# A two-block transformer on one core: GpSimd makes the gate's remainders between the strip transfers

## The reference, cut to what matters

```python
    u = u_tab[e]
    a = jax.nn.gelu(jnp.einsum('pd,phkd->phk', xb, u).astype(jnp.float32), approximate=False)
    return jnp.einsum('phk,phkd->pd', g * a, v_tab[e].astype(jnp.float32)).astype(xb.dtype)
```

## Time and profile before

| | |
|---|---|
| three runs | 3113.87 us median (3100.89 to 3116.61) |
| the profiled execution | 3107.74 us, of which the span is 3106.1 us |
| granted TensorE clock, mean | 0.951 of full |
| busy in the span | PE 92%, DVE 64%, ACT 34%, POOL 28% |
| stage V of layer 0, 727 to 1203 us | PE busy 456.8 of 476 us, DVE 384.7, POOL 45.6 |

### The profile page before, as it was taken

How to read it: one execution, slowest core, us unless ns; L and a number is a source line. 1 busy time by engine, 2 the same in 40 slices (tenths; PEclk the granted TensorE clock), 3 DMA queues, 4 the chain that set the end, 5 groups by cost and what they waited for, 6 DMA issues and landing times.

```text
span 3106.1 us, 54274 instructions
## 1 busy us (share of the span) xinstructions
PE 2857.3 (92%) x20018; PEld 2589.8 (83%) x20018; DVE 1981.1 (64%) x2912; ACT 1048.4 (34%) x1508; POOL 867.7 (28%) x521
## 2 busy tenths in 40 slices
PE   4989999999999988889999999999898879978798
PEld 4459999999999987669999999999896459855696
DVE  6433986777988766426967768997772349132690
ACT  1214443333333333224443333333342124321443
POOL 2006991000000110037970000001110029900596
PEclk9989999999999989889999999999998989987899
DMA  8524554445666874244554445667882335531454
GB/s 326 184 88 151 180 178 153 140 141 180 203 195 229 286 272 165 68 133 155 180 174 141 139 149 191 200 203 262 281 279 100 102 109 176 190 114 36 134 181 145
DMA packets 147037, 536.77 MB, mean 173 GB/s; under 512 B 16720, under 2 KB 17104, under 8 KB 146144
## 3 DMA queue, kind: packets, MB, share of 16 engines
q1 hardware_dynamic: 113936, 412.89, 40.1%
q0 software_dynamic: 30528, 113.26, 10.8%
q10 hardware_dynamic: 2448, 8.91, 0.7%
HBM read 531.85 MB, written 3.15 MB: 172 GB/s over the span
## 4 chain that ended last, share of the span: by engine, by line
PE 78%; DMA 7%; DVE 6%; issue 4%; POOL 3%; ACT 2%; SPq 0%; POOLq 0%; DVEq 0%; ACTq 0%
PE ps L1291 18%; PE ps L956 13%; PE ps L535 9%; PE ps L1261 7%; PE ps L960 7%; PE ps L1866 6%; DMA mod_w<-in_mod 5%; PE ps L1835 4%; POOL split_lo L1011 3%; PE ps L510 2%; PE ps L915 2%; PE ps L1839 2%; DVE mod_acc L371 2%; PE ps L1420 1%; PE ps L334 1%
## 5 line engine op out<-in xcount | busy, mean ns | idle before, releaser
L998 ACT ACTIVATE split_hi<-ring 128x1024 fp32r<-128x1024 f32 x672 | 706.9, 1053 | 754.4 <-PE ps L960 508.2
L1011 POOL TENSOR_TENSOR split_lo<-ring,split_hi 128x1024 fp32r<-128x1024 f32 x288 | 751.3, 2624 | 496.6 <-ACT split_hi L998 488.9
L1023 DVE TENSOR_TENSOR split_lo<-ring,split_hi 128x1024 fp32r<-128x1024 f32 x384 | 468.8, 1221 | 141.6 <-ACT split_hi L998 136.9
L351 POOL DMA_DIRECT2D mod_w<-in_mod x176 | 93.4, 531 | 1336.5 <-DVE mod_acc L371 721.0
L1291 PE MATMUL ps<-gate_lo,split_hi 128*128 128x256 f32 x2048 | 298.9, 290 | 27.6 <-DVE gate_lo L1021 27.6
L995 ACT ACTIVATE gate_hi<-gate 128x256 fp32r x256 | 106.8, 417 | 607.8 <-PE ps L1291 599.1
L1291 PE MATMUL ps<-gate_hi,split_hi 128*128 128x256 f32 x2048 | 299.9, 290 | 0.0
L1291 PEld LDWEIGHTS ps<-gate_lo,split_hi 128*128 128x128 f32 x2048 | 273.4, 198 | 30.8 <-DVE gate_lo L1021 30.8
L1291 PE MATMUL ps<-gate_hi,split_lo 128*128 128x256 f32 x2048 | 296.2, 289 | 0.0
L956 PE MATMUL ps<-hT_hi,split_hi 128*128 128x256 f32 x2048 | 292.5, 285 | 4.0 <-ACT split_hi L998 4.0
L960 PE MATMUL ps<-hT_hi,split_lo 128*128 128x256 f32 x2048 | 289.4, 284 | 3.0 <-POOL split_lo L1011 2.7
(11 more groups left out here) (290 smaller groups left out, 3567.0 us busy)
## 6 DMA issues: line engine op xcount, KB each, us to landing
ring<-in_stream SPq DMA_DIRECT2D x782, 512.0 KB, 4.1
mod_w<-in_mod POOLq DMA_DIRECT2D x176, 512.0 KB, 4.8
gate<-in_mod POOLq DMA_DIRECT2D x32, 512.0 KB, 8.4
gate<-in_mod ACTq DMA_DIRECT2D x16, 512.0 KB, 8.9
x_kept<-x POOLq DMA_DIRECT2D x2, 1024.0 KB, 4.1
x<-x_kept POOLq DMA_DIRECT2D x2, 1024.0 KB, 5.0
x<-in_x SPq DMA_DIRECT2D x1, 1024.0 KB, 4.8
out_x<-x SPq DMA_DIRECT2D x1, 1024.0 KB, 4.8
```

The source lines that it names most:

```text
L998: nc.scalar.activation(split_hi[:, e, :], ring[:, slot, e * D:(e + 1) * D], ACT.Copy).then_inc(hi_made, 1)
L1011: nc.gpsimd.tensor_tensor(split_lo[:, e, :], ring[:, slot, e * D:(e + 1) * D], split_hi[:, e, :].bitcast(F32), ALU.subtract).then_inc(lo_m ...
L1023: nc.vector.tensor_tensor(split_lo[:, e, :], ring[:, (START[name] + j) % RING, e * D:(e + 1) * D], split_hi[:, e, :].bitcast(F32), ALU.sub ...
```

## The change

Line 1021 leaves VectorE. `strip_loads_gpsimd` is replaced by a function that makes both `gate_lo` tiles of a slab on GpSimd and then issues that slab's transfers. GpSimd's new order is: load of chunk 0; then for slabs 0 to 31, two remainders and the load of the next slab's chunk; for slabs 32 to 55, two remainders, the load of this slab's second chunk, and the load of the next slab's first chunk; for slabs 56 to 63, two remainders and the next slab's chunk. The remainders keep the two waits (`hi_made`, `lo_free`) they had on VectorE; the loads keep theirs (`mod_used`). ScalarE, TensorE and SyncE run the same lists.

```diff
-        def strip_loads_gpsimd(pool, l):
+        def strips_and_gate_lo_gpsimd(pool, l):
+            before = l * LOOP_STRIPS * DC
+            def load(i, step, off):
+                if not isinstance(i, int) or i or off > 1 or l:
+                    pool.wait_ge(mod_used, i * step + (before + off - 1))
+                pool.dma_start(mod_slots[off % 2], io["mod"][bass.ds(i * step + (FIRST_STRIPS * DC + before + off), 1), :, :]
+                               .rearrange("a p n -> (a p) n")).then_inc(mod_landed[off % 2], 16)
+            def gate_lo_slab(i, j):
+                for e in range(2):
+                    tile = TILE0[f"v{l}"] + 2 * j + e
+                    pool.wait_ge(hi_made, i * 16 + (tile + 1))
+                    pool.wait_ge(lo_free, i * 16 + (tile + 1))
+                    nc.gpsimd.tensor_tensor(gate_lo[:, e, :], at(gate, i, 16 * SEQ, (2 * j + e) * SEQ, SEQ),
+                                            gate_hi[:, e, :].bitcast(F32), ALU.subtract).then_inc(gate_lo_made, 1)
+            def one_each(i):
+                for j in range(8):
+                    gate_lo_slab(i, j)
+                    load(i, DC, j + 1)
             pool.wait_ge(u_drained, (l + 1) * 68)
-            for k in range(DC):
-                if l or k >= 2:
-                    pool.wait_ge(mod_used, l * LOOP_STRIPS * DC + k - 1)
-                load(0, k)
-            with pool.Fori(1, LOOP_STRIPS) as i:
-                for k in range(DC):
-                    pool.wait_ge(mod_used, i * DC + (l * LOOP_STRIPS * DC + k - 1))
-                    load(i, k)
+            load(0, DC, 0)
+            one_each(0)
+            with pool.Fori(1, 4) as i:
+                one_each(i)
+            with pool.Fori(4, 7) as i:
+                for j in range(8):
+                    gate_lo_slab(i, j)
+                    for q in range(2):
+                        load(i, 2 * DC, 2 * j + q + 33 - 64)
+            for j in range(8):
+                gate_lo_slab(7, j)
+                if j < 7:
+                    load(7, DC, 81 + j - 7 * DC)
...
@@ split_lo_vector
-            if name in ("v0", "v1"):
-                nc.vector.tensor_tensor(gate_lo[:, e, :], at(gate, i, 16 * SEQ, (2 * j + e) * SEQ, SEQ),
-                                        gate_hi[:, e, :].bitcast(F32), ALU.subtract).then_inc(gate_lo_made, 1)
```

More of the change, by code:

```diff
@@ L345, in first_mod_tensor @@
             free[bank] = [f"first_strip{strips[1]}"]
-        def strip_loads_gpsimd(pool, l):
-            def load(i, k):
-                pool.dma_start(mod_slots[k % 2], io["mod"][bass.ds(i * DC + ((FIRST_STRIPS + l * LOOP_STRIPS) * DC + k), 1), :, :]
-                               .rearrange("a p n -> (a p) n")).then_inc(mod_landed[k % 2], 16)
-            pool.wait_ge(u_drained, (l + 1) * 68)
-            for k in range(DC):
-                if l or k >= 2:
-                    pool.wait_ge(mod_used, l * LOOP_STRIPS * DC + k - 1)
-                load(0, k)
-            with pool.Fori(1, LOOP_STRIPS) as i:
-                for k in range(DC):
-                    pool.wait_ge(mod_used, i * DC + (l * LOOP_STRIPS * DC + k - 1))
-                    load(i, k)
+        def strips_and_gate_lo_gpsimd(pool, l):
[16 more added lines that the diff above has]
+                    load(i, DC, j + 1)
+            pool.wait_ge(u_drained, (l + 1) * 68)
+            load(0, DC, 0)
[11 more added lines that the diff above has]
+                    load(7, DC, 81 + j - 7 * DC)
@@ L2137, in _ @@
                 split_lo_gpsimd(g, f"u{l}", 0, 8)
-                strip_loads_gpsimd(pool, l)
+                strips_and_gate_lo_gpsimd(pool, l)
                 g.wait_ge(*when(f"peer{l}.full"))
```

## The result

The changed kernel takes 3189.43 us (median of four runs, 3182.69 to 3200.77) against 3115.24 us before: the ratio is 1.0247, 95% interval 1.0197 to 1.0297. It was forecast at 3174 us, slower by 1.9%, in a range from 3130 to 3215.

A forecast was written before the change was run, and what follows sets the result against it. It took TensorE, with VectorE's nearly equal cycle, to bound slabs 0 to 31 and the chunks slabs 32 to 55. (12 + 18) x 2 layers = 60 us gave 3167.7 us profiled, 3174 us median (+1.9%), range 3130 to 3215.

The forecast's parts named there:

- First stretch: Stage V, slabs 0 to 31: waits between VectorE and GpSimd lengthen each slab by 0.4 us, +12 us per layer.
- rival 1: In V the engines do not hold each other up, only slabs 32 to 55 cost: 3146 us; chance 0.20.
- Second stretch, the load behind the remainder: Slabs 32 to 55: second chunk's load queues behind tile 1's remainder; 3.1 us at 6 strips, +18 us per layer.
- What the remainder itself adds there: Slabs 32 to 55: one 0.65 us engine wait per slab, counted only as upper end, 15.6 us per layer.
- the two cycles of other slabs: Slabs 32 to 55: slot cycle 7.04 us for two chunks, engine-and-load cycle 14.1 for two slabs; equal, nothing added.
- rival 2: Both stretches of V at their upper ends, TensorE more often at its lower clock: +124 us, 3238 us; chance 0.11.
- TensorE gets back nothing.: Slabs 32 to 55: 2.4 us per layer regained at `gate_lo` waits, taken away by remainders before `split_lo`; counted nothing.
- Last eight slabs: Slabs 56 to 63, one chunk each: the load goes out one slab ahead; cost nothing, or 1 us.
- Rival 3: TensorE's `gate_lo` waits in V vanish and nothing takes their place: faster, 3089 us; chance 0.05.

The follow-up runs named there:

- the memset: The changed kernel with a GpSimd memset of `gate_lo` in place of the remainder, its product left out: 3148.39 us, 1.0158 to the kernel before.
- the waits alone: The changed kernel with VectorE making all remainders; GpSimd keeps its order and its waits before the loads: 3149.91 us, 1.0141 to the kernel before.
- GpSimd in slabs 32 to 63 only: The changed kernel with remainders on GpSimd only in slabs 32 to 63, on VectorE in slabs 0 to 31: 3173.40 us, 1.0188 to the kernel before.
- half-width run: The changed kernel with 128x128 remainders on GpSimd in slabs 32 to 55, the other half not made: 3185.91 us, 1.0250 to the kernel before.

## Why the prediction was right, and where it was off

- *Direction and total.* Slower was forecast, +60 us on the profiled execution and +1.9%; measured were +74 us by the medians, +2.5%. That the total comes so near is in part luck: the forecast's +24 us for the first stretch did not come, and 28 us came from a term that it had put at nothing.
- *First stretch, forecast +12 us per layer (from -2 to +28).* Measured -1.0 and -1.6 us in the profiles, and 0.3% faster when it alone is changed. The mechanism is in the trace (`split_lo` 1440 ns on the mean against 1221 with the memset, the remainder 1.16 and 1.69 us against 0.72), and the rule of the Trainium skill that the forecast weighs (SBUF — State Buffer, "Who interferes with whom") agrees with the trace. Two steps failed. The waits were priced too high on VectorE's side: only `split_lo` was lengthened, by 0.22 us on the mean, 0.44 us a slab and not 1.30, while the one-hot forms kept their means (685, 1219 and 702 ns against 683, 1218 and 684 before). And busy time was taken for period: the waits were added to VectorE's 7.1 us although only the instructions between `split_hi` of tile 1 and the last one-hot instruction lie on the chain. In the slab shown one meeting falls ahead of a wait of 0.48 us, the other beside the merge. The lower end of the range was the answer, and with it rival 1's first half.
- *Second stretch, the load behind the remainder, forecast +18 us per layer.* The kernel with the waits alone measures this term: 196.0 + 199.4 - 181.3 - 177.6 = 36.5 us in the profiles against the 36 forecast, 46 us by medians. The mechanism was right. That the size agrees is partly luck: 3.1 us in each of 6 slabs were forecast, and the load was held by `split_hi` 13 and 15 times, at 1.3 us of stretch each.
- *What the remainder itself adds there, forecast nothing (upper end +15.6 us per layer).* Measured 238.5 + 214.5 - 196.0 - 199.4 = 57.6 us in the profiles and 28 us by the medians (74.2 - 46.3); the changed kernel's profile is of its slowest execution, 11 us above the median, which is a part of the difference. This is the term that was mis-sized. The forecast priced the remainder at 0.65 us, and set the two cycles of other slabs equal (14.1 us for two slabs), so that it added nothing. But the remainder takes 1.69 us when `split_lo` has started first, and both are released by the same `hi_made`. A load goes out right behind such a remainder in every other slab, 13 times a layer: 13 x 1.69 = 22 us per layer is what that comes to by an estimate from these rows, if none of it is swallowed. From one such load to the next within a strip it is 17.1 to 18.4 us in layer 0 (1070.96 to 1088.02, 1190.77 to 1209.14), not 14.1. The half-width run fits: 0.97 of the 1.69 us is the wait, which does not shrink with the work.
- *TensorE's clock.* Named only in rival 2. In the changed kernel the granted clock of the stretch is 0.81 and 0.89. Layer 0, with the lower clock, takes 24 us more than layer 1 for the same work, and TensorE is busy 182.9 us of it against 171.3, so 11.6 of the 24 us are longer matmuls. In the kernel with GpSimd in slabs 32 to 63 only it is layer 0 that has all its strip sums at the upper level, and takes 215.5 us, as layer 1 does here. So layer 1's 214.5 us against 199.4 for the waits alone, 15 us, is nearer to what the remainder adds without a fall of the clock than layer 0's 42.5. A full separation no run gives: idle time and clock went down together.
- *"TensorE gets back nothing."* Its waits for `gate_lo` are gone, as forecast, and larger waits for `split_lo` and the strips took their place.
- *Last eight slabs, nothing or 1 us.* From the last sum of the stretch to the strip's last sum it took 51.0 and 47.9 us before (layers 0 and 1), and 50.9 and 49.7 after: within 2 us.
- *Rival 3* (faster) would have needed `split_hi` of tile 1 ready before the chunk two before is used. In the slab shown it is 2.7 us after (1044.83 against 1042.10).

## What to carry to other kernels

Before an instruction is moved onto an engine that issues transfers, ask what it waits for: every transfer behind it in that queue inherits the wait, and a transfer whose slot is on the critical cycle must stand ahead of it. The place of one load decided nearly all of the 2.5% here (1.0247 with it behind, 1.0020 with it between). Two instructions released by the same semaphore on two engines that hold each other up meet whenever both engines are free; look where the loser's delay lands (before a wait it is free, ahead of a transfer it is paid). And where two slots' cycle bounds a stretch, more slots can give more than relief of an engine: here 1.5% against 0.3%.

## What the runs showed of the hardware

- The time an instruction on GpSimd waits for VectorE is inside its recorded length. The remainder of 128x256 takes 0.72 us alone and 1.69 us when a two-operand `split_lo` has just begun; the one of 128x128 takes 0.45 and 1.41. The wait is 0.97 and 0.96 us.
- A GpSimd instruction that waits gets its turn after VectorE's current instruction, though VectorE has its next one ready, in the slab shown: at 946.22 it waited for line 1207 to end, and `split_lo`, the next on VectorE, took 1.77 us instead of 1.22.
- VectorE's merge (one operand from PSUM, one from SBUF) kept 0.68 us beside a reading GpSimd instruction, and `split_lo` kept 1.22 us beside a GpSimd memset.
- The 16 strip matmuls take 1.84 us at the upper clock level and 3.58 us at the lower; in layer 0 of the changed kernel all five sums from 1055 us on ran at the lower one (granted clock 0.50 in the first of them), each after 4.2 to 6.4 us of idle time. In layer 1 the first five sums of the stretch had no idle time just ahead of them, and ran at the upper one.
